# Two-layer GLA / sliding-window trunk with PEER experts: ten ring slots, eight kept strips, a smaller scratch area, all engine programs written out

## The chip, the core and the metric

The kernel runs on one core of one Trainium2 chip. The metric is the device time of one execution in microseconds. The span of a profile is the time from its first to its last recorded instruction.

## The reference, cut to what matters

512 tokens of width 1024 go through two layers. Each layer adds a token mixer (layer 0 gated linear attention, "gla"; layer 1 sliding-window attention, "swa") and then a PEER mixer, all in float32. The PEER mixer is what moves nearly all of the data: each token picks 128 experts out of 16384 (8 heads, 16 experts each), and for each pick reads one row of `u` and one row of `v`.

```python
def peer_ffn(h, w_q, sub_keys, u, v):        # per block of 128 tokens
    q = (xb @ w_q).reshape(BLK, PEER_HEADS, PEER_QDIM)
    s1 = einsum('thd,hkd->thk', q[..., :64], sub_keys[:, 0])
    s2 = einsum('thd,hkd->thk', q[..., 64:], sub_keys[:, 1])
    ...                                       # two top-16 lists, top 16 of their sums: e, softmax g
    a = gelu(einsum('thkd,td->thk', u[e], xb)) * g
    return einsum('thk,thkd->td', a, v[e])
```

## The kernel before, in words

**Stages.** The 512 tokens are 4 blocks of 128, so there are 8 stages (4 blocks by 2 layers). Stage s *serves* the 128 picks of its block. One pick is one gather of 128 rows of 8 KB (a `u` row and a `v` row side by side), 1 MB, into one slot of `ring`. Beside it, the same engines do the *prep* of the next stage: norm, projections, mixer, output projection, queries and choice of experts. Before stage 0 there is a start in which the first prep runs alone.

**Serving one pick.** GpSimd (POOL) issues the gather as soon as the slot is free (`used`); VectorE (DVE) takes the dot product of the `u` half with `h_now` (L1076); ScalarE (ACT) makes gelu, the coefficient and, for most picks, a diagonal matrix (L1330, L1333, L1343); TensorE (PE) multiplies the `v` half by that diagonal into `acc` (L1650, four matmul records of one pick) and so frees the slot. For the picks listed in `VECTOR`, DVE adds the `v` half to `side` instead (L1069). Each engine is in order. A table `AT` says beside which pick ("beat", 0 to 127 in a stage) each piece of the prep stands in each engine's program. A beat lasts some 2.6 us.

**Weights.** A layer's weights are strips of 1 MB (256 columns): 20 in layer 0 (0-3 q and k, 4-7 v, 8-11 r, 12-15 out, 16-19 the PEER queries pq), 13 in layer 1 (0-4 q and kv, 5-8 out, 9-12 pq). The first 9 (`RESIDENT`) are kept in SBUF for the whole layer. The others are loaded again for each block through one buffer, `stream`, in two cuts of 512 KB: the cut of strip n+1 is loaded when PE has used the same cut of strip n. SyncE (SP) issues these loads in order, and each waits for what PE has said (`FREED`, from `DONE`). In the start, when the ring is empty, the strips after the kept ones lie in the ring's slots.

**Small loads between them.** `GAIN_AT` and `KEYS_AT` say ahead of which streamed strip SP issues the norm weights (`ffn_gain`, 4 KB) and the keys (512 KB). `spread_gain` (L1598) spreads the norm weights over the partitions with four matmul records, and DVE uses them in `h2` (L889). It stood between out strips 2 and 3, in the very first prep ahead of out strip 0.

**POOL's program.** The gathers stood in loops, eight to a round. A round began with a copy of eight indices to `pick_now` (L654), from which the gathers read them.

**Scratch.** `arena` holds all short-lived tiles, 8192 floats per partition.

Of the kernel before, what the change touches and what calls it, by code (L numbers as in the profile page):

```python
# [9 lines left out]
U32 = mybir.dt.uint32  # L10
# [5 lines left out]
P = 128  # L16
# [17 lines left out]
SLOTS = 8  # L34
ROUNDS = PICKS // SLOTS
# [4 lines left out]
RESIDENT = 9  # L40
# [28 lines left out]
TENSOR = {kind: tuple(tuple(i for i in range(SLOTS) if i not in v) for v in of) for kind, of in VECTOR.items()}  # L69
FOLD_AT = 14  # L70


TURNS = {kind: sum(len(p) for p in of) for kind, of in TENSOR.items()}

# [6 lines left out]
def turns_before(s):  # L81

    return sum(TURNS[kind_of(n)] for n in range(s))

# [60 lines left out]
def opening(engine):  # L145
# [10 lines left out]
    "pe": ["h2T"] + [f"{w}{j}" for j in range(PARTS) for w in ("pq", "scores")],  # L156
# [85 lines left out]
def build(nc, x, positions, gain_mix, gain_ffn, strips0, strips1, w_lr, w_alpha, b_alpha, gla_gain,  # L242
# [5 lines left out]
    with ExitStack() as ctx:  # L248
# [8 lines left out]
        pick_now = sb("pick_now", [P, 2, SLOTS], U32)  # L257
# [11 lines left out]
        arena = sb("arena", [P, 8192])  # L269
# [19 lines left out]
        rope_now = sb("rope_now", [P, 2, ROPE_HALF])  # L289
# [8 lines left out]
        picks_copied = sem("picks_copied")  # L298
        started = sem("started")
# [42 lines left out]
        h_next = area(5 * D, D)  # L342
        g_v = area(0, HEADS_A, DV)
        g_r = area(1024, HEADS_A, DV)
        g_o = area(2048, HEADS_A, DV)
        hn = area(3072, KT, P)
        angle = area(7680, 4, BLOCKS, ROPE_HALF)
        posi = area(7744, BLOCKS).bitcast(I32)
        posf = area(7748, BLOCKS)
        invf = area(7752, ROPE_HALF)  # L350
        g_b = area(4096, HEADS_A, P)
        g_t = area(4608, HEADS_A, P)
        g_eb = area(5120, HEADS_A, P)
        g_enb = area(5632, HEADS_A, P)
        g_ef = area(6144, HEADS_A, P)
        g_qd = area(6656, HEADS_A, P)
        g_kinv = area(7168, HEADS_A, P)
        g_kf = area(7680, HEADS_A, P)
        walpha = arena[0:RANK, 5120:5632]
        attnT = area(5632, HEADS_A, P)  # L360
        state1 = area(2048, HEADS_A, DV)
        g_kft = area(4096, HEADS_A, DK)
        junk = area(2048, D)
        ffn_gain = arena[0:1, 5120:5120 + D]
# [4 lines left out]
        s_p = [area(2304 + 1024 * i, 4, 2 * P) for i in range(2)]  # L369
        s_kdup = area(4352, HEADS_KV, 2, HD)  # L370
        s_pT = [area(4352 + 1024 * i, 8, P) for i in range(2)]
        s_o = area(6400, HEADS_Q, HD)
        bias_in = arena[0:1, 4096:5376]
        bias_out = arena[0:1, 0:D]
        s_rope = area(7424, 4, HEADS_Q + HEADS_KV, ROPE_HALF)

        pqT = area(0, HEADS_P, P)
        c_rest = area(1024, 2 * PART, KEYS)
        cand = area(1536, PART, LISTED)
        cand_rest = area(1792, PART, LISTED)  # L380
        onehot = area(2048, 2, PART * TOPK * TOPK)
        keysT = area(4096, HEADS_P, KEYS)
        top = area(6144, 2 * HEADS_P, TOPK)
        topi = area(6400, 2 * HEADS_P, TOPK).bitcast(U32)
        place = area(6400, 2, HEADS_P, TOPK)
        topf = area(6656, 2 * HEADS_P, TOPK)
        best = area(6912, HEADS_P, TOPK)
        besti = area(7040, HEADS_P, TOPK).bitcast(U32)
        ab = area(7168, 2, HEADS_P, TOPK).bitcast(U32)
        abf = area(7424, 2, HEADS_P, TOPK)  # L390
        ef = area(7680, 2, HEADS_P, TOPK)
        gsm = area(7936, 2, HEADS_P)
# [35 lines left out]

        def began_by(eng, who, event):
            eng.wait_ge(chosen[who], HEAD_START[who].index(event) + 1)  # L430
# [17 lines left out]
        def beside(half, prep_parts):  # L448


            per = SLOTS // BEAT
# [18 lines left out]
        def _(sp):  # L470
# [7 lines left out]
            def load_block(prep):  # L478
# [4 lines left out]
                if isinstance(stage, int) and stage == 1:  # L483
                    sp.wait_ge(side_begun, 1)
                elif not (prep.first and prep.layer == 0):

                    sp.wait_ge(used[VECTOR[before(prep).kind][0][0]], (stage - 1) * ROUNDS + 2)
                if prep.layer == 1:
                    sp.wait_ge(stored, prep.p * 16 + 17)
                sp.dma_start(xc[:], src[bass.ds(prep.p * P, P), :]).then_inc(x_loaded, 16)  # L490
                if prep.layer == 0:
                    sp.dma_start(walpha, w_alpha).then_inc(small_loaded, 16)
                else:

                    said_by(sp, "pe", before(prep), "scores3")
                    sp.dma_start(bias_in, b_in).then_inc(small_loaded, 16)
# [5 lines left out]
            def load_kept_ahead(prep):  # L502

                said_by(sp, "pe", before(prep), "v")
                for n in range(AHEAD):

                    sp.wait_ge(used[0], (BLOCKS - 2) * ROUNDS + (AHEAD_AT + n + 1))
                    load_kept(prep, n)

            def load_kept_rest(prep):  # L510

                said_by(sp, "pe", prep, "q")
                for n in range(AHEAD, RESIDENT):
                    sp.wait_ge(used[0], (BLOCKS - 1) * ROUNDS + (REST_AT + n - AHEAD + 1))
# [1217 lines left out]
```

## Time and profile before

| | |
|---|---|
| median of 3 runs | 2940.16 us (2938.06 to 2944.21) |
| span of the profiled execution | 2939.0 us |
| instructions | 27902 |
| busy share of PE, DVE, ACT, POOL | 78%, 74%, 40%, 44% |
| moved by DMA | 1170.16 MB, mean 398 GB/s |

The rows are from one profiled execution. A row of a timeline gives start, duration, engine, line, operation, what it writes and reads, and in brackets how long the engine had been idle before it and what ended that. A row of the windows view gives the stretch and its length, then the busy time of each engine with its number of instructions, the granted TensorE clock (1.00 is full), the busy share of the DMA engines (it can read 1.01 or 1.02 when they are full) and the GB/s moved. "Landing" is the time from the issue of a transfer to its end.

### The profile page before, as it was taken

Reading aid. Unit: us, or ns where it says so; the run is one execution under the profiler, and the core shown is the slowest. Engines: PE = TensorE matmul, PEld = TensorE weight load, DVE = VectorE, ACT = ScalarE, POOL = GpSimd, SP = SyncE. Lnnn points to the kernel's source line nnn. Section 1 sums busy time; section 2 is a strip of 40 time slices with the busy share of each in tenths; the row PEclk is TensorE's granted clock in tenths of the full one; section 3 lists DMA queues with packets and bytes.
Section 4 is the critical chain, followed back from the end, with each engine's and each line's share of the span. In section 5 each row is a group of like instructions: output and inputs, shape, how many; then the busy total and the mean of one; then the engine's idle time right before and its main releaser. Section 6 shows DMA issues by size and latency. Waiting matters only on the chain.

```text
span 2939.0 us, 27902 instructions
## 1 busy us (share of the span) xinstructions
PE 2279.9 (78%) x7308; PEld 1206.3 (41%) x7308; DVE 2186.8 (74%) x5158; ACT 1182.4 (40%) x3443; POOL 1282.0 (44%) x1186
## 2 busy tenths in 40 slices
PE   8578787687887887787787878877788777886767
PEld 6535453354433544243443435433443434432222
DVE  2497768775878757796688877978779786887664
ACT  2144434343443433344444453435534454433333
POOL 0144334443355433454434544345434454355555
PEclk9789989999898998998899998989889898998889
DMA  6499999999999999999999999999999999999998
GB/s 253 150 401 421 404 362 422 420 421 389 413 410 421 421 393 412 421 411 421 414 382 402 421 421 416 392 403 417 421 406 392 405 421 421 391 411 422 422 422 359
DMA packets 170941, 1170.16 MB, mean 398 GB/s; under 512 B 19681, under 2 KB 19937, under 8 KB 36401
## 3 DMA queue, kind: packets, MB, share of 16 engines
q0 software_dynamic: 147456, 1073.81, 88.7%
q1 hardware_dynamic: 23344, 94.74, 8.2%
q8 instruction: 57, 0.93, 0.1%
q14 instruction: 84, 0.68, 0.1%
HBM read 1164.28 MB, written 4.19 MB: 398 GB/s over the span
## 4 chain that ended last, share of the span: by engine, by line
DMA 25%; DVE 15%; PE 12%; issue 6%; ACT 4%; POOL 3%; POOLq 0%; DVEq 0%; ACTq 0%; SPq 0%
DMA ring<-in_uv,pick_now 23%; PE acc L1650 7%; DVE ring L1076 5%; POOL ring L662 3%; PE ps L1448 3%; DVE side L1069 1%; DMA xc<-h 1%; ACT diag L1343 1%; DMA stream<-in_strips 1%; DVE arena L955 1%; ACT coef L1333 1%; DVE arena L936 1%; DVE arena L1026 1%; DVE arena L1030 1%; DVE arena L937 1%
## 5 line engine op out<-in xcount | busy, mean ns | idle before, releaser
L1650 PE MATMUL acc<-ring,diag 128*128 128x512 f32 x2988 | 1554.2, 663 | 487.9 <-ACT diag L1343 486.7
L662 POOL DMA_INDIRECT ring<-in_uv,pick_now x1024 | 1225.1, 1196 | 1514.3 <-PE acc L1650 1046.9
L1076 DVE CUSTOM_DVE_ANT_0 ring<-ring,h_now 128x1024 f32<-128x1024 f32 x1024 | 1237.3, 1223 | 518.5 <-DMA ring<-in_uv,pick_now 506.8
L1650 PEld LDWEIGHTS acc<-ring,diag 128*128 128x128 f32 x2988 | 586.3, 208 | 1316.9 <-ACT diag L1343 743.2
L1330 ACT ACTIVATE gelu<-dots 128x1 f32<-128x1 f32 x1024 | 206.1, 201 | 1253.9 <-DVE dots L1076 1252.4
L1069 DVE SCALAR_TENSOR_TENSOR side<-ring,coef,side 128x1024 f32<-128x1024 f32 x270 | 346.0, 1282 | 32.1 <-ACT coef L1333 32.0
L1343 ACT ACTIVATE diag<-ident,coef 128x128 f32<-128x128 f32 x747 | 300.0, 402 | 68.8 <-PE acc L1650 44.7
L1333 ACT ACTIVATE coef<-gate,gelu 128x1 f32<-128x1 f32 x1024 | 301.5, 294 | 33.2
L1448 PE MATMUL ps<-resident,actT 128*128 128x256 f32 x896 | 219.5, 402 | 0.0
L1448 PEld LDWEIGHTS ps<-resident,actT 128*128 128x128 f32 x896 | 177.1, 201 | 44.2 <-issue 19.6
L1435 PE MATMUL ps<-actT,stream 128*128 128x128 f32 x992 | 131.0, 294 | 28.5 <-DMA stream<-in_strips 24.3
L1435 PEld LDWEIGHTS ps<-actT,stream 128*128 128x128 f32 x992 | 127.9, 209 | 48.6 <-DMA stream<-in_strips 26.0
L1448 PE MATMUL ps<-stream,actT 128*128 128x256 f32 x336 | 87.0, 409 | 42.2 <-DMA stream<-in_strips 40.8
L654 POOL COPY pick_now<-pick 128x8 uint32 (+1 forms) x128 | 52.1, 407 | 119.3 <-DVE pick L1033 118.5
L1330 ACT ACT_TABLE_LOAD x77 | 98.8, 1283 | 1.6 <-DVE dots L1076 0.2
L1448 PEld LDWEIGHTS ps<-stream,actT 128*128 128x128 f32 x336 | 65.4, 201 | 69.7 <-DMA stream<-in_strips 37.1
L1396 PE MATMUL ps<-ident,arena 128*128 128x128 f32 x224 | 40.3, 338 | 58.2 <-DVE arena L889 22.4
L1076 DVE DVE_READ_ACCUMULATOR2_ANT dots<- 128x1 f32 x1024 | 84.4, 82 | 0.0
L1284 ACT ACTIVATE arena<-ps 128x256 f32<-128x256 f32 x32 | 12.2, 381 | 135.8 <-PE ps L1435 135.7
L1396 PEld LDWEIGHTS ps<-ident,arena 128*128 128x128 f32 x224 | 32.7, 175 | 82.9 <-DVE arena L889 28.6
L1422 PEld LDWEIGHTS ps<-actT,resident 128*128 128x128 f32 x512 | 62.0, 199 | 8.7 <-issue 6.0
L1422 PE MATMUL ps<-actT,resident 128*128 128x128 f32 x512 | 62.4, 283 | 2.3 <-ACT actT L1155 2.3
(193 smaller groups left out, 1429.5 us busy)
## 6 DMA issues: line engine op xcount, KB each, us to landing
stream<-in_strips SPq DMA_DIRECT2D x104, 512.0 KB, 8.2
resident<-in_strips SPq DMA_DIRECT2D x18, 1024.0 KB, 12.4
ring<-in_uv,pick_now POOLq DMA_INDIRECT x1024, 12.5
ring<-in_strips SPq DMA_DIRECT2D x8, 1024.0 KB, 19.6
arena<-in_keys SPq DMA_DIRECT2D x8, 512.0 KB, 7.7
xc<-in_x SPq DMA_DIRECT2D x4, 512.0 KB, 6.9
h<-arena SPq DMA_DIRECT2D x4, 512.0 KB, 11.2
xc<-h SPq DMA_DIRECT2D x4, 512.0 KB, 7.8
```

What stands on the lines that cost most here:

```text
L654: step(pool.tensor_copy(pick_now[:, half, :], pick[:, bass.ds((base + pair) * (2 * SLOTS) + (half * SLOTS - layer * BLOCKS * PICKS), SLOTS)]))
L662: pool.indirect_dma_start(ring[:, i, :], None, tables[layer], bass.IndirectOffsetOnAxis(ap=pick_now[:, half, i:i + 1], axis=0),).then_inc( ...
L1069: dve.scalar_tensor_tensor(side[:], ring[:, i, D:2 * D], coef[:, i:i + 1], (side if began else xc)[:], ALU.mult, ALU.add).then_inc(used[i], 1)
L1076: dve.tensor_tensor_reduce(ring[:, i, 0:D], ring[:, i, 0:D], h_now[:], 1.0, 0.0, ALU.mult, ALU.add, dots[:, i:i + 1]).then_inc(dotted, 1)
L1330: act.activation(gelu[:, i:i + 1], dots[:, i:i + 1], ACT.Gelu).then_inc(gelued, 1)
L1333: act.activation(coef[:, i:i + 1], gate[:, bass.ds(col, 1)], ACT.Copy, scale=gelu[:, i:i + 1]).then_inc(weighed, 1)
L1343: act.activation(diag[:, i % 4, :], ident[:], ACT.Copy, scale=coef[:, i:i + 1]).then_inc(diag_ready, 1)
L1396: i = pe.transpose(ps[:, k // 4, (k % 4) * P:(k % 4 + 1) * P], src[:, k, :], ident[:])
L1422: i = pe.matmul(ps[:, bank, (2 * side + c) * P:(2 * side + c + 1) * P], w[:, k, c * P:(c + 1) * P], actT[:, k, :], start=(k == 0), stop=(k ...
L1435: i = pe.matmul(ps[:, 2 + c, (j % 2) * P:(j % 2 + 1) * P], w[:, k, c * P:(c + 1) * P], actT[:, k, :], start=(k == 0), stop=(k == KT - 1))
L1448: i = pe.matmul(dst, actT[:, k, :], w[:, k, :], start=(k == 0 and bias is None), stop=(k == KT - 1))
L1650: m = pe.matmul(acc[:, b * 512:(b + 1) * 512], diag[:, i % 4, :], ring[:, i, D + b * 512:D + (b + 1) * 512], start=(r == 0 and i == tensor ...
```

## The change

The ring gets ten slots in place of eight. Batches of eight picks stay the unit of the work tables (`BATCH`), but a pick n now lies in slot n mod 10. The 16 KB per partition come from one kept strip (`RESIDENT` 9 to 8, 8 KB) and the scratch area (8192 to 6144 floats, 8 KB). So one more strip per block goes through `stream` (r0 in layer 0, out3 in layer 1). Tiles in the scratch area lie closer, which moves some loads behind later events: layer 1's `bias_out` behind `o3`, `walpha` behind the scores of the prep before. The loops of SP and POOL are written out, so that slots and indices are constants; the copies to `pick_now` and DVE's `rope_now` are gone. The norm weights are spread behind the four output strips in every prep, with an event `gain` of its own, for which DVE waits ahead of `h2`.

```diff
-SLOTS = 8
-ROUNDS = PICKS // SLOTS
+BATCH = 8
+ROUNDS = PICKS // BATCH
+SLOTS = 10
-RESIDENT = 9
+RESIDENT = 8
-DONE = ([None, None, "r", None, None, None, "y", "pq0", "pq1", "pq2", "pq3"],
-        ["pq0", "pq1", "pq2", "pq3"])
+SAYS = ({11: "r", 15: "y", 16: "pq0", 17: "pq1", 18: "pq2", 19: "pq3"},
+        {8: "y", 9: "pq0", 10: "pq1", 11: "pq2", 12: "pq3"})
+DONE = [[SAYS[layer].get(n) for n in range(RESIDENT, STRIPS[layer])] for layer in range(2)]
-GAIN_AT = (4, 1)
+GAIN_AT = (13 - RESIDENT, 10 - RESIDENT)
-KEYS_AT = (DONE[0].index("y") + 1, 1)
+KEYS_AT = (16 - RESIDENT, 10 - RESIDENT)
...
+def pick_number(s, r, i):
+    return (s * ROUNDS + r) * BATCH + i
...
-    "pe": ["h2T"] + [f"{w}{j}" for j in range(PARTS) for w in ("pq", "scores")],
+    "pe": ["gain", "h2T"] + [f"{w}{j}" for j in range(PARTS) for w in ("pq", "scores")],
...
-        arena = sb("arena", [P, 8192])
+        arena = sb("arena", [P, 6144])
...
+        def released(eng, n):
+            eng.wait_ge(used[n % SLOTS], n // SLOTS + 1)
...
                 if prep.layer == 0:
+                    if stage:
+                        said_by(sp, "pe", before(prep), "scores3")
                     sp.dma_start(walpha, w_alpha).then_inc(small_loaded, 16)
...
             def load_streamed(prep):
                 if prep.layer == 1:
-                    said_by(sp, "pe", prep, "qT")
+                    said_by(sp, "pe", prep, "o3")
                     sp.dma_start(bias_out, b_out).then_inc(bias_loaded, 16)
...
                     if n == GAIN_AT[prep.layer]:
-                        if prep.first and prep.layer == 0:
-                            said_by(sp, "pe", prep, "o")
-                            said_by(sp, "dve", prep, "state1")
-                        else:
-                            said_by(sp, "pe", prep, "oT")
+                        said_by(sp, "pe", prep, "oT")
                         sp.dma_start(ffn_gain, gain_ffn[prep.layer:prep.layer + 1, :]).then_inc(gain_loaded, 16)
...
             def gathers(s, layer, begin, end):
-                base = s * (ROUNDS // 2)
-                with pool.Fori(begin, end) as pair:
-                    for half in range(2):
-                        n = (base + pair) * 2 + half
-                        step.restart()
-                        step(pool.tensor_copy(
-                            pick_now[:, half, :],
-                            pick[:, bass.ds((base + pair) * (2 * SLOTS)
-                                            + (half * SLOTS - layer * BLOCKS * PICKS), SLOTS)]))
-                        for i in range(SLOTS):
-                            pool.wait_ge(used[i], n + 1)
-                            alone(pool, passed["pool"])
-                            pool.indirect_dma_start(
-                                ring[:, i, :], None, tables[layer],
-                                bass.IndirectOffsetOnAxis(ap=pick_now[:, half, i:i + 1], axis=0),
-                            ).then_inc(got[i], 16)
+                for i in range(begin, end):
+                    n = s * PICKS + i
+                    if n >= SLOTS:
+                        released(pool, n - SLOTS)
+                        alone(pool, passed["pool"])
+                    elif SAYS[0].get(RESIDENT + n, "r") not in ("r", "y", "pq0"):
+                        said_by(pool, "pe", Prep("gla", 0), SAYS[0][RESIDENT + n])
+                        alone(pool, passed["pool"])
+                    col = n - layer * BLOCKS * PICKS
+                    pool.indirect_dma_start(
+                        ring[:, n % SLOTS, :], None, tables[layer],
+                        bass.IndirectOffsetOnAxis(ap=pick[:, col:col + 1], axis=0),
+                    ).then_inc(got[n % SLOTS], 16)
...
                 r = root(prep, 1, v, "sqrt2")
+                said_by(dve, "pe", prep, "gain")
                 say(prep, "h2", dve.scalar_tensor_tensor(h_next, xc[:], r, two_banks(2, 3), ALU.mult, ALU.mult))
...
             def select(prep, at):
                 for n in range(4):
...
-                    if n == 2 and not (prep.first and prep.layer == 0):
-                        spread_gain(prep)
                 say(i)
+                spread_gain(prep)
                 yield at["h2T"]
```

## Rows read from the trace of the kernel before

**Rows 1.** The page: GB/s moved in 40 equal slices of the span, and all bytes.

```profile
GB/s 253 150 401 421 404 362 422 420 421 389 413 410 421 421 393 412 421 411 421 414 382 402 421 421 416 392 403 417 421 406 392 405 421 421 391 411 422 422 422 359
...
HBM read 1164.28 MB, written 4.19 MB: 398 GB/s over the span
```

**Rows 2.** Windows view, stages 0 to 6, then a stretch without prep.

```profile
126.67:503.00 376.33, 295.77 (x1016) 167.13 (x1016) 304.89 (x805) 149.13 (x428) 160.89 (x151) 0.91 0.99 401
503.00:864.00 361.00, 280.25 (x953) 154.08 (x952) 273.48 (x628) 144.45 (x421) 157.11 (x145) 0.94 1.00 411
864.00:1233.00 369.00, 287.22 (x951) 155.83 (x952) 271.64 (x616) 142.77 (x418) 151.02 (x144) 0.92 1.01 413
1233.00:1592.00 359.00, 279.83 (x872) 143.18 (x871) 281.03 (x697) 154.78 (x448) 159.40 (x146) 0.91 1.00 409
1592.00:1935.00 343.00, 276.57 (x871) 143.56 (x869) 275.12 (x663) 153.57 (x444) 153.35 (x144) 0.91 1.00 410
1935.00:2279.00 344.00, 272.36 (x869) 141.74 (x868) 273.09 (x661) 152.62 (x442) 161.29 (x144) 0.92 0.99 407
2279.00:2611.00 332.00, 266.31 (x859) 139.26 (x858) 263.37 (x617) 149.33 (x432) 153.88 (x141) 0.92 1.00 409
...
2650.00:2900.00 250.00, 170.27 (x288) 60.92 (x288) 163.78 (x251) 80.53 (x273) 146.09 (x113) 0.84 1.01 422
```

**Rows 3.** The page, DMA issues: count, KB each, median us to landing.

```profile
stream<-in_strips SPq DMA_DIRECT2D x104, 512.0 KB, 8.2
...
ring<-in_uv,pick_now POOLq DMA_INDIRECT x1024, 12.5
```

**Rows 4.** Windows view: one stage boundary, then the ends of four layer-1 preps.

```profile
2285.00:2300.00 15.00, 9.87 (x24) 4.04 (x24) 10.70 (x30) 10.11 (x29) 5.02 (x4) 0.77 0.87 346
...
1485.00:1540.00 55.00, 46.49 (x184) 26.50 (x184) 45.97 (x168) 22.35 (x60) 16.81 (x19) 0.92 0.94 369
1845.00:1910.00 65.00, 56.72 (x199) 28.93 (x199) 62.06 (x238) 29.79 (x83) 25.17 (x25) 0.97 0.97 390
2180.00:2230.00 50.00, 41.66 (x155) 22.17 (x154) 43.34 (x166) 19.43 (x55) 21.91 (x20) 0.93 0.92 354
2505.00:2600.00 95.00, 79.33 (x310) 44.32 (x309) 82.99 (x278) 41.50 (x113) 35.81 (x35) 0.98 0.99 390
```

**Rows 5.** The page, DMA queues: packets, MB, share of 16 engines.

```profile
q1 hardware_dynamic: 23344, 94.74, 8.2%
```

**Rows 6.** Timeline of PE in stage 1: r0, r1 and the two cuts of r2.

```profile
648.91 3.62 PE L1448 MATMUL ps<-resident,actT 128*128 128x256 f32 x16
652.37 3.62 PE L1448 MATMUL ps<-stream,actT 128*128 128x256 f32 x16
...
662.29 1.99 PE L1448 MATMUL ps<-stream,actT 128*128 128x256 f32 x8 [2.87 <-DMA stream<-in_strips]
665.90 1.99 PE L1448 MATMUL ps<-stream,actT 128*128 128x256 f32 x8 [1.62 <-DMA stream<-in_strips]
```

**Rows 7.** Timelines of SP and PE, end of the prep in stage 6.

```profile
2458.89 0.24 SPq L536 DMA_DIRECT2D arena<-in_gain_ffn  x1
...
2504.27 5.41 PE L1448 MATMUL ps<-resident,actT 128*128 128x256 f32 x16
2509.51 3.60 PE L1650 MATMUL acc<-ring,diag 128*128 128x512 f32 x8
2516.06 1.09 PE L1396 MATMUL ps<-ident,arena 128*128 128x128 f32 x8 [2.95 <-DVE arena L889]
```

**Rows 8.** Timelines of PE and POOL, start and first gathers.

```profile
80.79 3.77 PE L1598 MATMUL ps<-arena,ones 1*128 1x512 f32 x4
...
125.45 0.25 POOL L654 COPY pick_now<-pick 128x8 uint32<-128x8 uint32 x1 [118.50 <-DVE pick L1033]
126.67 1.12 POOL L662 DMA_INDIRECT ring<-in_uv,pick_now  x1 [0.97 <-POOL pick_now L654]
...
153.67 1.26 POOL L662 DMA_INDIRECT ring<-in_uv,pick_now  x1 [16.16 <-issue]
```

More of the change, by code:

```diff
@@ L448, in beside @@
         def beside(half, prep_parts):
-            per = SLOTS // BEAT
+            per = BATCH // BEAT
             done = 0
@@ L482, in load_block @@
                 stage = prep.p + BLOCKS * prep.layer
-                if isinstance(stage, int) and stage == 1:
+                if stage == 1:
                     sp.wait_ge(side_begun, 1)
-                elif not (prep.first and prep.layer == 0):
-                    sp.wait_ge(used[VECTOR[before(prep).kind][0][0]], (stage - 1) * ROUNDS + 2)
+                elif stage:
+                    released(sp, pick_number(stage - 1, 0, VECTOR[kind_of(stage - 1)][0][0]))
                 if prep.layer == 1:
                     sp.wait_ge(stored, prep.p * 16 + 17)
-                sp.dma_start(xc[:], src[bass.ds(prep.p * P, P), :]).then_inc(x_loaded, 16)
+                sp.dma_start(xc[:], src[prep.p * P:(prep.p + 1) * P, :]).then_inc(x_loaded, 16)
                 if prep.layer == 0:
+                    if stage:
+                        said_by(sp, "pe", before(prep), "scores3")
                     sp.dma_start(walpha, w_alpha).then_inc(small_loaded, 16)
@@ L576, in _ @@
             load_block(Prep("gla", 1))
-            with sp.Fori(0, BLOCKS - 2) as s:
+            for s in range(BLOCKS - 2):
                 preps(Prep("gla", s + 1), Prep("gla", s + 2))
@@ L583, in _ @@
             close(BLOCKS - 1, 0)
-            with sp.Fori(BLOCKS, STAGES - 2) as s:
+            for s in range(BLOCKS, STAGES - 2):
                 preps(Prep("swa", s - (BLOCKS - 1)), Prep("swa", s - (BLOCKS - 2)))
@@ L670, in _ @@
+            for s in range(BLOCKS):
                 stage(s, Prep("gla", s), 0)
-            with pool.Fori(BLOCKS, STAGES) as s:
+            for s in range(BLOCKS, STAGES):
                 stage(s, Prep("swa", s - BLOCKS), 1)
@@ L1526, in gla @@
                 turn(g_o.rearrange("p h (a t) -> p (h a) t", t=P))
-                if prep.first:
-                    spread_gain(prep)
                 yield from select(prep, at)
@@ L1640, in serve, with part @@
                 tensor = TENSOR[kind_of(s)]
-                def part(r, slots):
-                    if r == FOLD_AT and slots[0] == 0:
+                def part(r, picks):
+                    if r == FOLD_AT and picks[0] == 0:
                         fold(s, VECTOR[kind_of(s)])
-                    for i in slots:
+                    for i in picks:
                         if i not in tensor[r]:
                             continue
-                        pe.wait_ge(diag_ready, turns_before(s) + sum(len(p) for p in tensor[:r]) + tensor[r].index(i) + 1)
+                        n = pick_number(s, r, i)
+                        slot, turn = n % SLOTS, TURN_OF[n]
+                        pe.wait_ge(diag_ready, turn + 1)
                         for b in range(2):
-                            m = pe.matmul(acc[:, b * 512:(b + 1) * 512], diag[:, i % 4, :],
-                                          ring[:, i, D + b * 512:D + (b + 1) * 512],
+                            m = pe.matmul(acc[:, b * 512:(b + 1) * 512], diag[:, turn % 4, :],
+                                          ring[:, slot, D + b * 512:D + (b + 1) * 512],
                                           start=(r == 0 and i == tensor[0][0]), stop=True, skip_group_check=True)
-                        m.then_inc(used[i], 1)
+                        m.then_inc(used[slot], 1)
                 return part
```

200 lines of the change are left out of this document (98 added, 102 removed).

## The prediction

> **What bounds the kernel now.** I read the page's slices first: after the start, the GB/s stand at 421 or 422 in about half of them and dip to 382 or 393 once or twice per stage [rows 1]. The stretch at the end that has no prep beside it moves 422 GB/s for 250 us with the DMA engines full [rows 2]. So the kernel is bound by its bytes, at 422 GB/s, and what is lost is the start, the dips and the tail. The windows by stage size the dips: a stage of 376.3 us at 401 GB/s lost 376.3 x (1 - 401/422) = 18.7 us, and the next six 9.4, 7.9, 11.1, 9.8, 12.2 and 10.2 us [rows 2]. That is 79 us in all, each stage's in several pieces: it is what a deeper ring can win, and no more.
>
> Then why they dip. A gather takes 2.49 us of the engines (1.049 MB at 422 GB/s) and lands 12.5 us after its issue [rows 3], so of eight slots five are in transfer and three are held by the consumers. When PE or ACT stands still for over 12 us or so, POOL gets no slot and the engines drain. At the boundary of a stage, where ACT waits for the next block, 15 us run at 346 GB/s, a loss of 2.7 us [rows 4]. Two more slots are two more gathers in transfer, 2 x 2.49 = 5.0 us more cover for each stall.
>
> **The change part by part.**
>
> *More strips (cost).* One strip more is streamed in each prep but the first of each layer (there it is either loaded anyway as a kept strip or lies in the ring): 6 strips, 6.29 MB. At 422 GB/s that is 14.9 us. The SP queue moved 94.74 MB in 8.2% of 2939.0 us, 2.54 us per MB [rows 5], which gives 16.0. Bounds 14.9 and 16.0; I take **+15.5 us**, all of it on the path, because the bound is bytes.
>
> The Trainium skill ("DMA: Bandwidth & Descriptors", "Where 436 GB/s comes from") puts the HBM side at about 358 GB/s per core; by it the strips would be 17.6 us. The trace disagrees, with 422 GB/s held for 250 us [rows 2].
>
> *Two more slots (gain).* Two groups of dips. Those at the end of the layer-1 preps lose 55 x (1 - 369/422) = 6.9, 65 x (1 - 390/422) = 4.9, 50 x (1 - 354/422) = 8.1 and 95 x (1 - 390/422) = 7.2 us, 27 us [rows 4]; I set them aside, since the change adds a wait just there. The other 52 us are some 25 dips, like the boundary's 2.7 us, nearly all under the 5.0 us of cover. They aren't won whole: close dips share one cover, since the deeper queue must first fill again, and near them the consumers are not much faster than the DMA. Above, all 52; below, half, 26. I take **-37 us**, nearer to the upper end because 2.7 us is well inside 5.0.
>
> *A wait for r1 (layer 0).* r0 and r1 stand at one beat (56) and PE runs them back to back, at 648.91 and 652.37, since r0 was kept and r1 was loaded long before [rows 6]. Now r0 lies in the stream buffer and the first cut of r1 can be issued only when PE has used that of r0. The nearest row is r2: r1's first half was done near 654.2, and r2's cuts were there at 662.29 and, after 1.62 us more, at 665.90, that is 8.1 us from release to start [rows 6]. So r1 starts 6.3 us late (8.1 less the second half of r0, 1.8) and waits 1.6 us at its second cut: PE stands for some 8 us in preps 2 and 3, less in prep 1, where two beats lie between. Behind PE all `acc` matmuls queue, thus slots, thus POOL. Against it stand 5.0 us of new cover and 2.5 us in which the new strip itself fills the engines: 8 - 7.5 is about 0.5 us each. Above, with no cover left from the stall before, 5 each. **+2 us** (0 to 15). The spread of the norm weights, moved from ahead of out3 to behind it, also no longer hides in out3's wait for its strip: 2 us of PE each, in the same cover.
>
> *A wait for the norm weights (layer 1).* This is the part I think least provided for. `GAIN_AT` is now 2 in layer 1, so SP issues `ffn_gain` behind both cuts of strip 9, and the second cut waits for `y`, which PE says after out3. But `spread_gain` now follows `y` on PE. Before, SP issued it at 2458.89, over 50 us ahead of out3's end near 2509.6 [rows 7]. Now PE waits from `y` for a load issued after `y`, behind 1 MB on the same queue. A cut lands in 8.2 us in the median [rows 3]; with two issues ahead I take 8.5 us. Below it could be 3 us if the small load passes the cuts, above 11. What queues behind it on PE is the serving: after `y` it ran two picks at once, then waited 2.95 us for `h2` until 2516.06 [rows 7]. DVE's `h2` waits for `gain` too, so `h2T` comes 8.5 + 2 us after `y` in place of 6.5, 4 us later. Set against 7.5 us of cover the stall costs about 1 us in each of the four preps, but it uses the cover up, and the 27 us of dips that follow stay: **+4 us** (0 to 25), and nothing won from the 27 (a gain of up to 20 as the other end).
>
> *The start.* The very first spread (3.77 us from 80.79, half of it hidden by ACT's copy) stood ahead of out0 [rows 8]; without it out0 starts about 1.4 us sooner. The copy of the indices and its wait, from 125.45 to 126.67, goes from ahead of the first gather [rows 8]: -1.2. The ninth gather, now at once, was issued only at 153.67 [rows 8]; its gain is in the dips of stage 0. **-2.6 us** (0 to -4). All other copies lie behind a full queue: nothing. If that cover were gone, each would cost the 1.2 us of [rows 8] once in eight picks.
>
> *The rest.* `bias_out` behind `o3` (beat 68, needed at 75) and out3's strip (needed at 87) have 7 and 19 beats of 2.6 us against 8.2 us to land. `walpha` behind the old scores: those lie in the stage before, so SP passes at once. DVE's two copies go: nothing. SP's and POOL's written-out programs add instruction bytes that the trace of before can't price; between -2 and +3 us, I take 0.
>
> Sum: 15.5 - 37 + 2 + 4 - 2.6 = -18.1; span 2939.0 to about 2921. The median of the runs is 1.2 us above the span of the profile: **2922 us**.
>
> **The rivals.**
>
> *Most dips fill.* The norm-weight wait is short or falls on a full queue, and the 27 us are won as well: 15.5 - 47 - 15 - 2.6, that is some 2892 to 2908, middle 2900. For it: every single dip is below 5 us but those of layer 1's ends. Against it: the new waits lie exactly where the trace dips.
>
> *The new waits eat the cover.* PE stands 8 us in each of three gla preps and 10.5 us (with the spread) in each of four swa preps; if the queue is still short when they come, they cost 5 and 7 us, 15 + 28 = 43 us, against 37 + 15.5 - 2.6: 2940 + 15.5 - 37 + 43 - 2.6 = 2959; with half of that loss 2937 to 2945. It decides where the engines' queue holds less than the stall, that is if fewer than four gathers (10 us) are in transfer when `y` is said. For it: 354 GB/s at the end of one such prep [rows 4], so the queue is short there already.
>
> *Strips land later behind the deeper ring.* If a strip's cut shares one line with the gathers, ten slots put up to 5.0 us in front of each. PE then waits up to 5 us longer at some five cuts of each of seven preps, 175 us of PE, of which I let a fourth reach the end: 2922 + 44 = 2966. Against it: a cut lands in 8.2 us while a gather with the same engines takes 12.5 [rows 3], so it does not stand behind the gathers.
>
> The Trainium skill ("DMA: Bandwidth & Descriptors", "Queues, rings and completion order") says that each DMA engine goes round-robin over the queues with work, a packet at a time. By that, depth alone would not delay a strip and this rival would add nothing; the two landings agree.
>
> *The slots don't reach the engines.* POOL, or slots freed in order, keeps the number in transfer at five: only the costs stay, 2940 + 15.5 + 2 - 2.6 = 2955.
>
> **How the numbers follow.** Chances: forecast 0.48 (own range 2910 to 2936), most dips fill 0.20, waits eat the cover 0.22 (2937 to 2959), later strips 0.05, no reach 0.05. The range 2896 to 2948 takes in the second and the near half of the third, and leaves some 0.18 out. About 0.2% (5.9 us) is what a measurement of this kernel can tell from no change, so faster is below 2934.3 and slower above 2946.0. Faster: 0.44 + 0.20 = 0.64. Same: 0.04 + 0.12 = 0.16. Slower: 0.20.
>
> **What would show it.** Bytes 1176.5 MB, 110 stream loads; the page's slices nearer to 422 outside layer 1's prep ends; the windows by stage at 413 to 418 GB/s in layer 0. Gathers landing in up to 17.5 us. A PE wait of about 6 us for r1 at beat 56; a PE wait of 8 to 9 us at the L1598 group in layer 1, and DVE waiting there for PE ahead of `h2`. The boundary windows near 420 GB/s. The prediction is wrong if the gathers' landing stays at 12.5 us, if the strips' rises by over 2 us, or if the swa stages lose more than before.

## The result, and the profile after

| | before | changed |
|---|---|---|
| median of 20 runs | 2942.45 us | 2946.41 us |
| span of the profiled execution | 2939.0 us | 2941.9 us |
| moved by DMA | 1170.16 MB | 1176.54 MB |
| gathers, issue to landing (median) | 12.5 us | 16.7 us |

The ratio is 1.0015 with a 95% interval of 1.0008 to 1.0021: no change that matters, and if anything slower. One of the 20 runs of before took 7695.19 us; without it their median is 2942.09 us. 2922 us had been forecast, a gain of 0.6%.

The page of the changed kernel: GB/s in 40 equal slices, the SP queue, all bytes.

```profile
GB/s 267 148 409 421 416 368 420 421 421 396 395 420 421 418 373 407 421 422 421 421 377 421 421 421 413 402 421 421 421 388 416 421 422 420 372 421 421 421 422 350
...
q1 hardware_dynamic: 25080, 101.03, 8.8%
...
HBM read 1170.57 MB, written 4.19 MB: 399 GB/s over the span
```

The 6.3 MB of strips are there, and more slices stand at 421 than in [rows 1]. But the dips are as deep as before or deeper (373, 377, 372). The windows by stage answer to [rows 2]:

```profile
126.00:497.00 371.00, 296.93 (x1010) 169.54 (x1011) 301.54 (x797) 148.61 (x425) 163.04 (x135) 0.90 1.00 405
497.00:859.00 362.00, 278.45 (x955) 151.54 (x953) 272.11 (x622) 143.66 (x419) 157.85 (x130) 0.94 1.00 410
859.00:1236.00 377.00, 292.75 (x952) 158.13 (x952) 271.69 (x621) 143.55 (x419) 156.87 (x128) 0.90 1.00 408
1236.00:1586.00 350.00, 279.18 (x862) 144.33 (x863) 272.99 (x660) 152.14 (x441) 152.79 (x126) 0.89 1.00 412
1586.00:1927.00 341.00, 271.31 (x870) 141.71 (x869) 272.62 (x661) 152.92 (x443) 152.08 (x129) 0.90 1.00 415
1927.00:2268.00 341.00, 272.59 (x868) 143.91 (x867) 271.87 (x657) 152.37 (x441) 153.04 (x128) 0.90 1.00 413
2268.00:2613.00 345.00, 277.25 (x870) 145.30 (x870) 272.60 (x660) 152.96 (x442) 148.79 (x129) 0.89 0.99 411
```

With the prediction's rule, length x (1 - GB/s / 422), the seven stages lose 14.9, 10.3, 12.5, 8.3, 5.7, 7.3 and 9.0 us, 68 us against 79 before. So the ten slots won 11 us of the dips net, where 31 (37 less 6 for the new waits) had been forecast, and the strips cost 15. Nothing of it was won in the three stages with a layer-0 prep (37.7 us against 36.0), all of it in the four with a layer-1 prep (30.3 against 43.3), although these hold the wait for the norm weights.

The trace shows what became of the single stalls. The first fence is the windows view at three stage boundaries of layer 1, two rows of before and then three of the changed kernel; the second is the timeline of PE (r0 and r1 in stage 1, then the end of the prep in stage 6), the third that of SP:

```profile
1600.00:1615.00 15.00, 10.21 (x24) 4.04 (x24) 12.04 (x32) 10.59 (x31) 5.92 (x5) 0.77 0.83 335
1940.00:1955.00 15.00, 9.62 (x21) 4.80 (x22) 10.05 (x27) 9.43 (x26) 5.19 (x4) 0.66 0.83 332
...
1600.00:1615.00 15.00, 7.17 (x18) 3.10 (x18) 7.34 (x17) 7.21 (x18) 4.61 (x5) 0.66 1.02 422
1940.00:1955.00 15.00, 7.62 (x17) 3.54 (x16) 7.47 (x17) 6.87 (x16) 4.39 (x4) 0.63 1.01 421
2285.00:2300.00 15.00, 9.02 (x22) 4.35 (x23) 9.52 (x25) 9.24 (x26) 4.75 (x4) 0.66 1.02 425
```

```profile
646.12 3.62 PE L1446 MATMUL ps<-stream,actT 128*128 128x256 f32 x16
655.93 6.29 PE L1446 MATMUL ps<-stream,actT 128*128 128x256 f32 x16 [6.19 <-DMA stream<-in_strips]
...
2502.78 3.72 PE L1446 MATMUL ps<-stream,actT 128*128 128x256 f32 x16
2516.83 3.78 PE L1593 MATMUL ps<-arena,ones 1*128 1x512 f32 x4 [10.34 <-DMA arena<-in_gain_ffn]
2520.54 5.64 PE L1648 MATMUL acc<-ring,diag 128*128 128x512 f32 x8
2526.02 1.04 PE L1394 MATMUL ps<-ident,arena 128*128 128x128 f32 x8
```

```profile
2506.90 0.29 SPq L540 DMA_DIRECT2D arena<-in_gain_ffn  x1
```

The boundaries, at 335, 332 and 346 GB/s before (the third in [rows 4]), run full: the stall of ACT is still there (8.7 us in front of L1167 at the last one, 8.3 before), and two more gathers cover it. r1 waits 6.19 us. The norm weights are issued at 2506.90, 0.4 us after out3, and PE stands for 10.34 us in front of the spread. Before, it served two picks right after out3 [rows 7].

The first fence is the timeline of POOL around this wait, the second the windows view:

```profile
2501.07 1.28 POOL L660 DMA_INDIRECT ring<-in_uv,pick  x1 [1.20 <-DVE side L1067]
2525.13 0.94 POOL L660 DMA_INDIRECT ring<-in_uv,pick  x1 [22.79 <-PE acc L1648]
```

```profile
2510.00:2515.00 5.00, 0.00 (x0) 0.00 (x0) 2.17 (x8) 1.58 (x4) 0.00 (x0) 0.58 1.02 417
2515.00:2520.00 5.00, 3.17 (x4) 1.16 (x4) 0.00 (x0) 0.00 (x0) 0.00 (x0) 0.50 0.91 372
2520.00:2525.00 5.00, 5.00 (x7) 2.04 (x7) 3.66 (x5) 0.00 (x0) 0.00 (x0) 0.55 0.11 48
...
2505.00:2540.00 35.00, 22.06 (x85) 12.26 (x85) 18.58 (x43) 9.20 (x21) 8.16 (x7) 0.80 0.81 319
```

The queue was full when PE began to wait: until 2515 the DMA engines run at 417 GB/s, though POOL has issued nothing since 2502.4. Then they drain, because POOL's own pause is longer than PE's wait: 22.79 us, most of it out3 (3.72), the wait (10.34) and the spread (3.78). The spread takes 3.78 us at a granted clock of 0.50 to 0.55 (the level of 1.2 GHz); before it took 1.98. Over the 35 us of the last row a quarter of the bytes is missing: 35 x (1 - 319/422) = 8.5 us lost in one dip, with ten slots.

### The profile page after: what moved, and what is told of

Same layout as the page of the kernel before. It is cut to its first block, busy times and chain, and to the rows that moved or that the text cites. A ratio compares the mean times of both kernels' runs of the same rounds, so it can differ in the third digit from the quotient of the medians.

```text
span 2941.9 us, 27005 instructions
## 1 busy us (share of the span) xinstructions
PE 2283.9 (78%) x7308; PEld 1214.6 (41%) x7308; DVE 2180.4 (74%) x5150; ACT 1182.6 (40%) x3443; POOL 1268.2 (43%) x1049
## 2 busy tenths in 40 slices
DMA packets 172687, 1176.54 MB, mean 400 GB/s; under 512 B 19876, under 2 KB 20136, under 8 KB 38136
## 4 chain that ended last, share of the span: by engine, by line
DMA 36%; DVE 23%; PE 17%; issue 6%; ACT 5%; POOL 2%; SPq 0%; POOLq 0%; DVEq 0%; ACTq 0%
DMA ring<-in_uv,pick 28%; DVE ring L1076 9%; PE acc L1648 8%; DMA stream<-in_strips 5%; PE ps L1446 5%; POOL ring L660 2%; DVE side L1067 2%; DMA arena<-in_gain_ffn 1%; DVE arena L1022 1%; DVE arena L1026 1%; PE ps L1433 1%; DVE arena L951 1%; ACT diag L1341 1%; DVE arena L932 1%; DMA xc<-h 1%
## 5 line engine op out<-in xcount | busy, mean ns | idle before, releaser
L660 POOL DMA_INDIRECT ring<-in_uv,pick x1024 | 1263.8, 1234 | 1645.3 <-PE acc L1648 1091.2
L1648 PE MATMUL acc<-ring,diag 128*128 128x512 f32 x2988 | 1537.1, 659 | 427.8 <-ACT diag L1341 427.0
L1333 ACT ACTIVATE coef<-gate,gelu 128x1 f32<-128x1 f32 x1024 | 302.0, 295 | 33.3
L1446 PE MATMUL ps<-resident,actT 128*128 128x256 f32 x768 | 185.4, 398 | 0.0
L1446 PE MATMUL ps<-stream,actT 128*128 128x256 f32 x448 | 124.7, 434 | 60.4 <-DMA stream<-in_strips 59.3
L1446 PEld LDWEIGHTS ps<-resident,actT 128*128 128x128 f32 x768 | 150.1, 199 | 38.1 <-issue 17.7
L1433 PE MATMUL ps<-actT,stream 128*128 128x128 f32 x960 | 123.4, 289 | 31.8 <-DMA stream<-in_strips 29.5
L1433 PEld LDWEIGHTS ps<-actT,stream 128*128 128x128 f32 x960 | 119.4, 203 | 48.8 <-DMA stream<-in_strips 31.5
L1446 PEld LDWEIGHTS ps<-stream,actT 128*128 128x128 f32 x448 | 93.4, 216 | 97.4 <-DMA stream<-in_strips 50.5
L1394 PE MATMUL ps<-ident,arena 128*128 128x128 f32 x224 | 40.4, 340 | 41.8 <-DVE arena L702 22.8
L1420 PEld LDWEIGHTS ps<-actT,resident 128*128 128x128 f32 x512 | 64.1, 205 | 10.9 <-issue 7.0
L1593 PE MATMUL ps<-arena,ones 1*128 1x512 f32 x32 | 24.8, 915 | 41.7 <-DMA arena<-in_gain_ffn 41.7
## 6 DMA issues: line engine op xcount, KB each, us to landing
ring<-in_uv,pick POOLq DMA_INDIRECT x1024, 16.7
```

The costliest lines, as they stand in the source:

```text
L660: pool.indirect_dma_start(ring[:, n % SLOTS, :], None, tables[layer], bass.IndirectOffsetOnAxis(ap=pick[:, col:col + 1], axis=0),).then_in ...
L1333: act.activation(coef[:, slot:slot + 1], gate[:, col:col + 1], ACT.Copy, scale=gelu[:, slot:slot + 1]).then_inc(weighed, 1)
L1394: i = pe.transpose(ps[:, k // 4, (k % 4) * P:(k % 4 + 1) * P], src[:, k, :], ident[:])
L1420: i = pe.matmul(ps[:, bank, (2 * side + c) * P:(2 * side + c + 1) * P], w[:, k, c * P:(c + 1) * P], actT[:, k, :], start=(k == 0), stop=(k ...
L1433: i = pe.matmul(ps[:, 2 + c, (j % 2) * P:(j % 2 + 1) * P], w[:, k, c * P:(c + 1) * P], actT[:, k, :], start=(k == 0), stop=(k == KT - 1))
L1446: i = pe.matmul(dst, actT[:, k, :], w[:, k, :], start=(k == 0 and bias is None), stop=(k == KT - 1))
```

## The experiments

**Theory A**: a slot's cover works as forecast, and the new waits, together with the streamed strip, use it up. **Theory B**: slots are worth little, since the consumers are too slow where the DMA dips. Further ones (C, D, E) stand where they came up. "Norm weights early" is one edit used in several:

```diff
-GAIN_AT = (13 - RESIDENT, 10 - RESIDENT)
+GAIN_AT = (13 - RESIDENT, 9 - RESIDENT)
```

| run | slots, kept strips (two numbers: layer 0 and layer 1) | edit | median us | against before (95%) |
|---|---|---|---|---|
| the change | 10, 8 | | 2946.41 | 1.0015 (1.0008 to 1.0021) |
| e1 | 10, 8 | norm weights early | 2934.64 | 0.9981 (0.9971 to 0.9991) |
| e2 | 10, 8 | e1, spread ahead of out3 | 2934.39 | 0.9982 (0.9972 to 0.9991) |
| e3 | 8, 8 | | 3002.1 | 1.0218 (1.0197 to 1.0238) |
| e4 | 9, 9 | | 2917.47 | 0.9925 (0.9910 to 0.9940) |
| e5 | 8, 9 | | 2944.5 | 1.0003 (0.9993 to 1.0013) |
| e6 | 8, 8 | norm weights early | 2969.43 | 1.0088 (1.0074 to 1.0103) |
| e7 | 10, 8 | e2, r1 later | 2934.88 | 0.9971 (0.9960 to 0.9982) |
| e8 | 9, 9 | spread ahead of out3 | 2920.21 | 0.9921 (0.9908 to 0.9934) |
| e9 | 9, 8 | norm weights early | 2943.9 | 1.0005 (0.9996 to 1.0014) |
| e10 | 10, 9 | ninth strip's load left out | 2907.03 | 0.9880 (0.9865 to 0.9895) |
| e11 | 9, 9 | the strip's bytes, no waits | 2931.33 | 0.9971 (0.9959 to 0.9982) |
| e12 | 9, 8 | e9, r1 later | 2942.18 | 1.0004 (0.9994 to 1.0014) |
| e13 | 9, 8 and 9 | e9, out3 not streamed | 2931.8 | 0.9975 (0.9964 to 0.9985) |
| e14 | 9, 9 and 8 | e9, r0 not streamed | 2925.05 | 0.9949 (0.9936 to 0.9963) |

Each row is measured beside runs of the kernel before, whose median is 2942.0 us for e1 to e4, 2943.3 for e5 to e8, 2942.6 for e9 to e11, 2940.1 for e12 and 2940.7 for e13 and e14. The differences below are of the medians of the third column; by the intervals of the last column one such difference is good to some 4 us, and to some 7 where e3 is in it.

**e1, norm weights early.**

> The changed kernel with one edit: the norm weights of layer 1 are issued one strip earlier, ahead of both cuts of strip 9, so no longer behind the event y. Theory A (the new waits eat the cover): PE's waits for the norm weights in layer 1 (41.7 us in four) go, and of the some 25 us that the four prep ends of layer 1 lose against 421.5 GB/s about half comes back: 8 to 12 us below the changed kernel, some 2936 us. Theory B (the deeper ring is worth little because the consumers are too slow there anyway, and the waits are beside the point): within 3 us of the changed kernel.

11.8 us below the change by the medians, 10 by the ratios. The timelines of SP and PE in stage 6 of this run show why:

```profile
2450.25 0.25 SPq L540 DMA_DIRECT2D arena<-in_gain_ffn  x1
```

```profile
2497.35 3.72 PE L1446 MATMUL ps<-stream,actT 128*128 128x256 f32 x16
2501.00 1.98 PE L1593 MATMUL ps<-arena,ones 1*128 1x512 f32 x4
2502.91 3.70 PE L1648 MATMUL acc<-ring,diag 128*128 128x512 f32 x8
```

The load is out 50 us ahead, the spread follows out3 without a pause and takes 1.98 us, and two picks are served next. In the windows of 5 us from 2495 to 2530 this run moves 416 GB/s or more, through the place where the changed kernel falls to 48. Theory A's number; the wait was worth 10 to 12 us and one digit takes it away.

**e2, the spread ahead of out3 again.** The call goes back into the loop at n == 2, the event `gain` and DVE's wait for it go.

> As e1_gain_early, and the spread of the norm weights stands between out strips 2 and 3 again, in every prep, without an event of its own. Theory A: in layer 0 the 2 us of the spread hide in the wait for out3's strip again, so that the stretch in which PE frees no slot is 2 us shorter in each prep; 2 to 5 us below e1_gain_early. Theory B: the same as e1_gain_early.

The same as e1. Theory A was wrong on this point: 2 us of PE per prep, some 12 us earlier (at 728.35 in stage 1, at 740.30 in e1), make no difference that can be seen.

**e3, eight slots.** `SLOTS = 8`.

> The changed kernel with eight slots in place of ten and all else kept, eight kept strips, the waits for r1 and for the norm weights too. In the start the strips pq0 to pq3 are then streamed, which the trace will show apart (some 8 us later first gather). Theory A: the two slots cover the stalls, so without them each of the seven preps loses up to 5.0 us twice: 25 to 45 us above the changed kernel with the start taken off. Theory B: the slots are worth little: under 10 us above it with the start taken off.

56 us above the change, more than theory A's upper end, and far from theory B's 10. The first gather comes at 125.93 (125.19 in the change), so the start has no part in it.

**e4, nine slots and nine kept strips.** `SLOTS = 9`, `RESIDENT = 9`.

> The changed kernel with nine slots and nine kept strips, which take the same memory: no strip more than before is streamed (1170 MB), neither r1 nor the norm weights wait, and the cover is 2.5 us. Theory A: the 15 us for bytes are saved, the new stalls are gone, and half the old dips are covered: some 2922 us (2915 to 2928). Theory B: about the kernel before less the start, 2936 to 2941 us.

24.5 us below before and 29 below the change: the best of the kernels that compute everything. The forecast for theory A, 2915 to 2928, holds. Windows by stage of this run, stages 1, 2 and 4:

```profile
496.00:855.00 359.00, 284.99 (x952) 156.91 (x952) 272.84 (x623) 144.34 (x421) 150.20 (x129) 0.92 1.01 412
855.00:1224.00 369.00, 285.41 (x952) 154.93 (x952) 272.70 (x621) 144.07 (x420) 153.02 (x129) 0.93 1.01 415
...
1571.00:1908.00 337.00, 271.19 (x868) 141.63 (x866) 272.18 (x657) 152.23 (x440) 151.82 (x129) 0.92 1.01 416
```

By the same rule they lose 8.5, 6.1 and 4.8 us. The changed kernel lost 10.3 and 12.5 us in the two stages with a layer-0 prep, more than before (9.4 and 7.9), and 5.7 in the third (9.8 before). So the tenth slot did not make up for the streamed r0.

**e5, eight slots and nine kept.** What is left of the change is its text: written-out programs, small scratch area, later spread.

> The changed kernel with eight slots and nine kept strips: what is left of the change is the written-out programs, the smaller scratch area and the norm weights behind out3 (issued before y, since with nine kept strips they stand one strip earlier). If the 56 us that e3_slots8 lies above the changed kernel are the price of the two slots' loss on top of the streamed strip and its waits (theory A), this run is near the kernel before, 2936 to 2944 us, and the streamed strip with its waits costs some 60 us at eight slots. If the written-out programs or the scratch area cost something by themselves (theory C), it lies at 2950 us or above.

Equal to before (1.0003). Theory C falls: the written-out programs, the scratch area and the later spread together neither cost nor gain. It also makes e5 the right base, and e3 lies 58 us above it: that is what one strip streamed more costs at eight slots, with its bytes, its waits and the wait for the norm weights.

**e6, e3 with the norm weights early.**

> e3_slots8 with the norm weights of layer 1 issued one strip earlier, as in e1. It prices the wait for the norm weights at the old depth. Theory A: four waits of 10.3 us with no cover to spare, 25 to 40 us below e3_slots8, some 2970 us. Theory B: the waits lie under other waits, under 10 us below it, 2992 us or more.

32.7 us below e3. The four waits (9.65 to 10.49 us in e3, 10.20 to 10.61 in the change) cost 32.7 us at eight slots and 11.8 at ten, 8.2 and 3.0 us each. The difference is 5.2 us a wait (good to 2 us), near the 2 x 2.49 = 5.0 us of cover that the prediction gave to two slots. What is left above e5 is 24.9 us; less the bytes (13.9, see e11), the waits of the streamed strip cost 11.0 us at eight slots.

**e7, r1 later.** On top of e2, with the beats of preps 2 and 3 in layer 0:

```diff
-"r0": 56, "r1": 56, "r2": 60, "upd": 62, "r3": 62, "o0": 64, "o1": 64,
+"r0": 56, "r1": 59, "r2": 61, "upd": 63, "r3": 64, "o0": 65, "o1": 65,
```

> e2_gain_ahead with r1 three beats behind r0 in layer 0's preps 2 and 3 (r1 59, r2 61, upd 63, r3 64, o0 and o1 65). Theory A: PE's wait of 6.2 us for r1 after r0 shrinks to under 1 us, and the deeper ring's cover is free for the out strips: 2 to 6 us below e2, some 2930 us. Theory B: the same as e2 within 2 us.

The medians of e2 and e7 are equal (2934.4 and 2934.9), so theory A fails here. See e12.

**e8, e4 with the spread ahead of out3.**

> e4_nine_nine with the spread of the norm weights between out strips 2 and 3 again and no event for it. Theory A: 2 to 5 us below e4, 2912 to 2916 us. Theory B (the place of the spread does nothing, as e2 against e1): 2916 to 2919 us.

Against before it is at 0.9921, e4 at 0.9925: no effect of the place of the spread can be seen here either, and theory A fails.

**e9, nine slots, eight kept, norm weights early.**

> The changed kernel with nine slots, eight kept strips and the norm weights of layer 1 issued one strip earlier. It stands between e6 (eight slots, 2969 us) and e1 (ten slots, 2935 us). If the worth of a slot falls with each one added, as dips run out, the ninth takes more than half of the 35 us: 2944 to 2950 us. Against e4 (nine slots, nine kept, 2917.5 us) it prices the streamed strip at nine slots: theory A says more than its 15 us of bytes, 25 to 32 us; theory D (only the bytes cost, since the waits fall under others) says 15 to 18 us, thus 2933 to 2936 us.

With eight kept strips the ninth slot is worth 25.5 us (e6 to e9) and the tenth 9.3 (e9 to e1). Against e4 the streamed strip costs 26.4 us. The two slots together bring 34.8 us here, and 55.7 (e3 to the change) where the wait for the norm weights is in place: the stalls of that wait are covered on top of the old dips, not in their stead (20.9 us more, good to some 8).

**e10, ten slots and nine kept, in imitation.** The ninth kept strip's tile and loads don't exist; its products use the eighth's data, so r0 and out3 are computed from other weights.

```diff
-        resident = sb("resident", [P, RESIDENT, KT, STRIP])
+        resident = sb("resident", [P, RESIDENT - 1, KT, STRIP])
...
-                return resident[:, n]
+                return resident[:, min(n, RESIDENT - 2)]
```

> Ten slots and nine kept strips, which doesn't fit in memory; so the ninth kept strip is left out and its products are computed with the data of the eighth. Left out are also the two loads of that strip into the kept tile, 2 MB, some 5 us. It prices two slots with no strip streamed more. Theory A (the cover works at ten slots too, and what takes it away in the change is the streamed strip): 2900 to 2910 us, 33 to 43 us below the kernel before. Theory B' (the tenth slot is worth nothing, since the losses left are no longer for want of slots): 5 us below e4, 2912 us or above.

2907.0 with 2 MB left out. At e11's price (13.9 us for 6.29 MB, 2.2 us per MB) these are 4.6 us, so 2911.6 us: two slots without a streamed strip are worth 33 us against e5, the ninth 27 and the tenth 6. That is theory A's size for both; the tenth's 6 us alone are hardly clear of the noise.

**e11, the bytes without the waits.** A 1 MB copy to a spare tensor in HBM, for which no engine of the kernel waits:

```diff
+                if not prep.first:
+                    ...
+                    sp.dma_start(spare, strips[prep.layer][8]).then_inc(spared, 16)
```

> e4_nine_nine with 1 MB more moved in each prep but the first of each layer, from a strip to a spare tensor in HBM, which nobody waits for: the bytes of the streamed strip (6.29 MB) without its waits. Theory A: 15 to 17 us above e4, some 2933 us; what e9 lies above this run is then the price of the waits. Theory D: the same, and e9 equal to this run within 3 us. If a byte in the gaps is free (the engines do not bind), 2918 to 2923 us.

13.9 us above e4, next to the 14.9 us of the bytes at 422 GB/s. The copy goes from HBM to HBM and stands ahead of the prep's first streamed strip, so it imitates the strip's load without being the same transfer. So 12.6 of e9's 26.4 us are not bytes, and theory D falls. PE's idle time in front of strips grows with the streamed strip: summed over the run, it is 65.6 us in e4, 71.3 in e11 and 85.5 in e9.

**e12, e9 with r1 later.**

> e9_slots9_gain_early with r1 three beats behind r0, as in e7, but at nine slots, where less cover can hide the wait. e9 lay 12.6 us above e11, which moves the same bytes without the waits of the streamed strip. Theory A (PE's wait of 6 us for r1 in two preps is what these 12.6 us are): 2932 to 2937 us. Theory E (they are elsewhere, in the streamed out3 and the queries behind it in layer 1, or spread over all strips since more strips come through one buffer): 2941 to 2945 us.

1.7 us below e9 (1.0004 against 1.0005 of before): nothing, theory E. Yet the wait for r1 did shrink. Timelines of PE in stage 1, first of e9, then of this run, r0 to r3:

```profile
645.38 3.62 PE L1446 MATMUL ps<-stream,actT 128*128 128x256 f32 x16
655.17 6.49 PE L1446 MATMUL ps<-stream,actT 128*128 128x256 f32 x16 [6.18 <-DMA stream<-in_strips]
...
681.67 1.99 PE L1446 MATMUL ps<-stream,actT 128*128 128x256 f32 x8 [0.28 <-DMA stream<-in_strips]
```

```profile
647.00 3.62 PE L1446 MATMUL ps<-stream,actT 128*128 128x256 f32 x16
650.45 3.60 PE L1648 MATMUL acc<-ring,diag 128*128 128x512 f32 x8
656.84 1.99 PE L1446 MATMUL ps<-stream,actT 128*128 128x256 f32 x8 [2.79 <-DMA stream<-in_strips]
660.60 1.99 PE L1446 MATMUL ps<-stream,actT 128*128 128x256 f32 x8 [1.77 <-DMA stream<-in_strips]
...
666.73 1.99 PE L1446 MATMUL ps<-stream,actT 128*128 128x256 f32 x8 [2.42 <-DMA stream<-in_strips]
670.86 1.99 PE L1446 MATMUL ps<-stream,actT 128*128 128x256 f32 x8 [2.14 <-DMA stream<-in_strips]
...
681.81 1.99 PE L1446 MATMUL ps<-stream,actT 128*128 128x256 f32 x8 [1.80 <-DMA stream<-in_strips]
```

PE serves two picks after r0, and then waits at r1, r2 and r3 all the same. From the start of r0 to the end of r3 it takes 36.8 us, against 38.3 in e9 (645.38 to 683.66) and, where r0 is kept, 33.3 in e4 (644.98 to 678.30) and 30.6 in the kernel before (648.91 to 679.55). Summed over the run, PE's idle time in front of strips is 83.9 us in 42 waits, and 85.5 in 42 in e9: the wait was moved, not removed. The strips pass through one buffer, each load starting when the strip before it is used, so a strip more is a load more in the chain; a later beat for r1 did not shorten it.

**e13 and e14, the streamed strip in one layer alone.** e9 with the number of kept strips by layer, (8, 9) and (9, 8), and the ninth replaced by the eighth's data as in e10 (1 MB of loads less each).

> e9 (nine slots, norm weights early), but in layer 1 out3 is not streamed: its load is left out and its products are computed with the data of the kept strip before it. So only layer 0 streams one strip more (r0). 1 MB of the first load is left out too. If the waits lie in layer 0, this is near e9 less the bytes of three strips and of that load, 10 us: 2932 to 2935 us. If they lie in layer 1, they go as well: 2919 to 2924 us. If they are spread, between.

> The mirror of e13: in layer 0 r0 is computed with the data of the kept strip before it and its load is left out, in layer 1 out3 is streamed. If the waits lie in layer 0: 2919 to 2924 us. If they lie in layer 1 (out3 and the queries behind it come one after another through the one buffer): 2932 to 2935 us.

With the 1 MB put back (2.3 us), e13 is at 2934.1 and e14 at 2927.4, which is 16.6 and 9.9 us above e4: together 26.5, as e9 has it (26.4). Each layer's three strips are 7.0 us of bytes. So the waits are some 9.6 us in layer 0 and 2.9 in layer 1, each good to 4 or 5 us. Both medians lie just outside the bands for "all in layer 0" (2932 to 2935, 2919 to 2924), on the side of "spread": most of the waits are in layer 0, not all, as the windows of the change had it too (10.3 and 12.5 us lost in two layer-0 stages, 8.5 and 6.1 in e4). There r1, r2, r3 and the out strips already came one behind the other; that this is the reason is argued, not shown.

## Why the prediction was wrong, step by step

*Bound by bytes, 422 GB/s.* Right. e11 prices 6.29 MB at 13.9 us; +15.5 was forecast.

The Trainium skill's 358 GB/s per core on the HBM side ("DMA: Bandwidth & Descriptors", "Where 436 GB/s comes from") had given 17.6 us. It is not what binds in this kernel, which runs on one core: the windows hold 421 to 425 GB/s, and e11's bytes cost 13.9 us.

*Two slots, -37 us.* Right in size: -33 with nine kept strips (e5 to e10), -35 with eight (e6 to e1). Wrong in shape: the ninth slot brings 25 to 27 us and the tenth 6 to 9. The prediction valued cover by the depth of each dip and did not ask what the first half of it leaves for the second; that dips of some 2 to 3 us leave little to a second slot of 2.5 us is the likely reason, argued and not shown.

*The streamed strip's waits, priced as the wait for r1, +2 us.* This is the step whose mechanism failed: "5.0 us of new cover and 2.5 us in which the new strip itself fills the engines: 8 - 7.5 is about 0.5 us each". The wait itself was foreseen to 0.1 us (6.3, measured 6.19). But beyond their bytes the strip's waits cost 11.0 us at eight slots (e6), 12.6 at nine (e9 less e11) and 9.1 at ten (e1 less e10's 2911.6 and the 13.9 of bytes): within the noise the same at every depth, so the two new slots took little or nothing off them. And they are not the wait for r1: e7 and e12 moved it and gained nothing. What the runs show is a longer chain of loads. From r0 to r3 PE needs 38.3 us with r0 streamed (e9) and 33.3 with r0 kept (e4; 30.6 before), and its idle time in front of strips grows by 17 to 20 us in a run whatever the depth (64.1 to 83.6 at eight slots, 65.6 to 85.5 at nine, 73.2 to 90.6 at ten). Why cover doesn't help against this chain stays open.

*The wait for the norm weights, +4 us.* Right mechanism and place, mis-sized: 11.8 us. The step that failed is the length, "I take 8.5 us": the four waits are 10.4 us. The prediction's rule for cover holds: 10.4 less its 7.5 us is 2.9 us a wait, 11.7 us in four. e6 shows the price without the two slots, 32.7 us. The margin was thin, so 2 us more of wait tripled the cost.

*The start, -2.6 us.* The first gather is issued at 125.19 in place of 126.67, 1.5 us earlier, and e5 shows nothing of it in the time.

*Text, 0.* Right (e5).

From 2922 to 2946.4 us, then: 4 us because the base is e5's 2944.5 and not 2940.2, 4 for the slots, -2 for the bytes, 7 for the strip's waits, 8 for the norm weights and 3 for the start. The sum closes by construction, since its parts are differences of the same medians; it confirms nothing, it says where the error lies. Most of it, 15 of 24 us, are the two waits.

In time, what came is near the rival "the new waits eat the cover", with half of its loss (2937 to 2945), 1.4 us past the upper end. The two waits cost 20.9 us, half of its 43, and the 43.7 us at eight slots (e3 less e5 less the bytes, 57.6 - 13.9) are its whole sum, split otherwise: 11.0 and 32.7 in place of 15 and 28. But its mechanism is not what the trace shows. It asked for a queue with less than 10 us in transfer when PE says `y`, and quoted 354 GB/s for it. In the changed kernel (stage 6) the engines move 417 GB/s for over 8 us after that point and 372 in the 5 us behind, and the norm-weight stalls got their cover in full. So that the time came near it is in part luck.

*The signs.* Bytes, the gathers' landing (16.7 us), r1's wait and the boundaries came as written. The number of stream loads is 116; the 110 there is a slip (six strips of two cuts are 12 more than 104). The sign that failed is "413 to 418 GB/s in layer 0": the three stages with a layer-0 prep run at 405, 410 and 408. None of the three signs for "wrong" came: the landing grew, the strips' did not, the stages with a layer-1 prep lost less than before. They did not reach the step that failed.

*The rival of later strips.* The page of four runs, landing of strips and, for three, of gathers: eight slots (e3), nine (e4), ten (e1), then the strips of the change itself (ten).

```profile
stream<-in_strips SPq DMA_DIRECT2D x120, 512.0 KB, 8.0
...
ring<-in_uv,pick POOLq DMA_INDIRECT x1024, 12.5
```

```profile
stream<-in_strips SPq DMA_DIRECT2D x102, 512.0 KB, 8.4
...
ring<-in_uv,pick POOLq DMA_INDIRECT x1024, 14.7
```

```profile
stream<-in_strips SPq DMA_DIRECT2D x116, 512.0 KB, 9.8
...
ring<-in_uv,pick POOLq DMA_INDIRECT x1024, 17.3
```

```profile
stream<-in_strips SPq DMA_DIRECT2D x116, 512.0 KB, 8.1
```

The gathers' landing grows by what the slots add. The strips' does not in the change (8.1 us, 8.2 before); with the norm weights early it is 9.8 (e1 and e2), and why is open. The rival's 5 us a cut didn't come: PE's idle time in front of strips is 87.9 us in e3 and 88.8 in the change, 83.6 in e6 and 90.6 in e1, at most 7 us more in the whole run for two slots. So later strips are at most a small part of why the tenth slot is worth less than the ninth.

By the Trainium skill ("DMA: Bandwidth & Descriptors", "Queues, rings and completion order"), with the engines going round the queues a packet at a time, depth alone would not delay a strip. The 8.1 us of the change agree; the 9.8 of e1 and e2 don't.

## What to carry to other kernels

Measure a stall where it counts: not the consumer's wait alone, but the time until the buffer's issuer can issue again (10.3 us of PE were 22.8 us of POOL here). When a wait is only a little longer than the cover, its length must be known well: 10.4 us in place of 8.5 made 3 us of 1. And don't set cover against a chain of loads through one buffer: a load more in it cost 9 to 13 us beyond its bytes at eight, nine and ten slots alike.

Price memory by trying the splits: here the same 8 KB lie in a tenth slot (2946.4 us, or 2934.6 with the norm weights early) or in a ninth kept strip (2917.5 us, 0.9925), and nine and nine beat both kernels. When a load is moved behind an event, look for who waits for it and whether that one waits right after the event; here one index in a table was worth 10 to 12 us.

## What the runs showed that was not expected

Two kinds of stall behave differently under a deeper ring. The same four waits for the norm weights, 41 us of PE standing still, cost 32.7 us of time at eight slots and 11.8 us at ten, 5 us less each, the worth of two gathers. The waits of the streamed strip cost 9 to 13 us at eight, nine and ten slots. And it matters little where in its prep a strip waits (e7, e12), or a 2 us matmul group stands (e2, e8), while an 8 us load more in the chain costs some 3 us in each prep of layer 0, beyond its bytes.
